# A hybrid attention and gated-linear-attention layer on eight cores: other scrap pairs and transfer order, and one exponential for two maps

## What is computed

```python
h = rms_norm(x, g_pre)
qa, ka, va, za, qb, kb, vb, zb, lr, gate_a, gate_b = split(h @ w_in)   # 5648 columns
# mixer A: 4 heads, two maps m of 64 dims each, causal, ALiBi
p = softmax(q_m k_m^T / 8 - slope * dist)              # m = 0, 1
oa = rms_norm((p_0 - lam * p_1) @ va, g_sub_a) * (1 - lam_init)
ya = (oa * silu(za)) @ w_up_a
# mixer B: gated linear attention, 4 heads, state S (64 x 128)
S_t = diag(alpha_t) S_{t-1} + k_t^T v_t;  ob = q_t S_t  # alpha from lr @ w_alpha
yb = (rms_norm(ob, g_sub_b) * silu(zb)) @ w_up_b
y = sigmoid(gate_a) * ya + sigmoid(gate_b) * yb
out = x + rms_norm(y @ w_out, g_post)
```

## Time and profile before

| | us |
|---|---|
| median of 3 runs | 1646.62 |
| lowest and highest of them | 1643.45, 1820.38 |
| the profiled execution | 1651.65 |
| its span on the slowest core (core 1) | 1650.0 |
| spans of all cores | 1627.0 to 1650.0 |
| PE busy | 1430.6 (87%) |
| ACT busy | 852.6 (52%) |
| DVE busy | 711.4 (43%) |
| POOL busy | 465.3 (28%) |

### The profile page before, as it was taken

One profiled execution on the slowest core, in us unless ns is written; L12 is line 12 of the kernel. 1 busy time (PEld: TensorE's weight loads), 2 busy tenths in 40 slices (PEclk: granted clock), 3 DMA queues, 4 the chain that ended last, 5 costly groups with the idle time before them and its releaser, 6 DMA issues.

```text
span 1650.0 us, 27769 instructions; the slowest of 8 cores (1627.0 to 1650.0 us)
## 1 busy us (share of the span) xinstructions
PE 1430.6 (87%) x10576; PEld 747.7 (45%) x10576; DVE 711.4 (43%) x1449; ACT 852.6 (52%) x1714; POOL 465.3 (28%) x469
## 2 busy tenths in 40 slices
PE   4868687899899997999879998799997999987888
PEld 2324333444445543555445554455543555543443
DVE  3546645653565343542435324353233441242434
ACT  4244343434453555355464665646666657666632
POOL 1024422253225221432204322043311240220342
PEclk9888889999999998999989999999999999999999
DMA  9966487423542335222442223422234312223113
GB/s 286 236 194 179 133 272 233 141 90 115 192 141 90 103 115 179 90 90 93 156 134 66 90 90 122 162 75 76 80 101 153 98 59 76 78 91 115 52 65 115
DMA packets 75437, 207.43 MB, mean 126 GB/s; under 512 B 7984, under 2 KB 26672, under 8 KB 75312
## 3 DMA queue, kind: packets, MB, share of 16 engines
...
## 4 chain that ended last, share of the span: by engine, by line
PE 60%; DVE 12%; ACT 10%; DMA 9%; issue 3%; POOL 3%; SPq 2%; DVEq 0%; POOLq 0%; ACTq 0%
PE ps_q L270 30%; PE ps_f L270 18%; PE ps_oa L270 12%; DMA out<-sb_scr 4%; ACT sb_PT L964 4%; DMA sb_KT<-w_in 3%; DVE sb_scr L841 2%; SPq L364 1%; ACT sb_junk L859 1%; ACT sb_ztmp L613 1%; DVE sb_scr L861 1%; DVE sb_wring L377 1%; DVE sb_rz L990 1%; DMA sb_KT<-w_out 1%; DVE sb_tmpo L992 1%
## 5 line engine op out<-in xcount | busy, mean ns | idle before, releaser
L964 ACT ACTIVATE sb_PT<-ps_q 128x512 bf16<-128x512 f32 (+3 forms) x685 | 363.0, 568 | 254.8 <-PE ps_q L270 170.7
L270 PE MATMUL ps_oa<-sb_V,sb_PT 128*128 128x129 bf16 x4224 | 345.8, 222 | 15.1 <-ACT sb_PT L964 7.5
L270 PEld LDWEIGHTS ps_oa<-sb_V,sb_PT 128*128 128x128 bf16 x4224 | 287.1, 99 | 143.4 <-issue 35.2
L964 ACT ACTIVATE sb_PT<-ps_f 128x512 bf16<-128x512 f32 (+3 forms) x467 | 255.6, 564 | 150.5 <-PE ps_q L270 75.1
L270 PE MATMUL ps_q<-sb_hT,sb_wring 128*128 128x512 bf16 x1040 | 267.3, 391 | 26.0 <-ACT sb_wring L373 8.6
L270 PE MATMUL ps_q<-sb_QT,sb_KT 64*128 64x512 bf16 (+3 forms) x685 | 163.7, 368 | 45.1 <-ACT sb_scr L636 20.5
L270 PE MATMUL ps_f<-sb_hT,sb_wring 128*128 128x512 bf16 x752 | 189.3, 386 | 5.9 <-ACT sb_hT L591 3.7
L809 POOL TENSOR_TENSOR sb_yT<-sb_scr 128x512 bf16<-128x512 f32 x64 | 81.2, 1270 | 397.1 <-DVE sb_scr L807 397.1
L270 PE MATMUL ps_q<-sb_wring,sb_hT 128*128 128x512 bf16 x616 | 166.6, 407 | 21.4 <-DVE sb_szA L614 12.3
L270 PEld LDWEIGHTS ps_q<-sb_hT,sb_wring 128*128 128x128 bf16 x1040 | 94.8, 100 | 141.2 <-issue 62.5
L270 PE MATMUL ps_f<-sb_QT,sb_KT 64*128 64x512 bf16 (+3 forms) x467 | 134.5, 364 | 16.4 <-DVE sb_yT L614 3.1
...
## 6 DMA issues: line engine op xcount, KB each, us to landing
sb_wring<-wsc SPq DMA_DIRECT2D x204, 512.0 KB, 3.6
sb_xb<-x SPq DMA_DIRECT2D x60, 512.0 KB, 4.5
...
out<-sb_scr SPq DMA_DIRECT2D x32, 512.0 KB, 3.3
wsc<-sb_wring SPq DMA_DIRECT2D x30, 512.0 KB, 6.0
...
```

The source lines that it names most:

```text
L270: P.op("pe", lambda e: e.matmul(out=out_, lhsT=lhsT, rhs=rhs, start=start, stop=stop, **kw), reads=reads, writes=writes)
L964: act(lambda e, pp=pp, m=m, c0=c0, b=b, cbias=cbias: e.activation(out=PT[pp][:, m, c0:512], in_=BANK[b][:, c0:512], func=AF.Exp, bias=cbia ...
```

## The change

1. **Pairs.** Group s of the output projection uses pair (s + 2) % 3 instead of s % 3: pairs 2, 0, 1, 2.
2. **Order at the end of `u_f`.** `fin(3)` comes first, then `release(4)`.
3. **Scratch stores.** `wsc` stores are no longer issued behind the conversion, but when the slot is loaded the next time (`owed`), seven pieces later.
4. **Start.** The `cstB` loads go behind six weight pieces, `setup_small` behind K of tile 1; only 8 x loads are issued in the start, the next three and the gpost load at the end of tile 0's attention.
5. **Tile 1.** The core units of the linear attention get cost factor 2 and gaps of 0.5.
6. **Banks.** PSUM is now two pairs of neighbouring banks (q0 with q1, q2 with q3) and one bank f. `bank_take` takes f if two takes have passed since its last, else the one idle for longest. `emit_qk` needs both pairs: a loop runs units on until they are free. Block kb uses one pair for its two maps, the pair idle for longer first.
7. **Exponential.** One activation for each key block reads both banks (2 x 512 columns, on the diagonal 2 x fewer) and writes both maps.

```diff
-        psQ = [PSM(f"q{i}", [128, 512], F32) for i in range(3)]
-        psF = [PSM(f"f{i}", [128, 512], F32) for i in range(2)]
+        psQ = [PSM(f"q{i}", [128, 1024], F32) for i in range(2)]
+        psF = PSM("f", [128, 512], F32)
...
         def bank_take():
-            return idle_banks.pop(0)
+            b = idle_banks[0]
+            if "f" in idle_banks and turn["n"] - turn["f"] >= 2:
+                b = "f"
+            idle_banks.remove(b)
+            turn["n"] += 1
+            turn[b] = turn["n"]
+            return b
...
+        def pair_free(i):
+            return f"q{2 * i}" in idle_banks and f"q{2 * i + 1}" in idle_banks
+
+        def pair_order():
+            age = [max(idle_banks.index(f"q{2 * i}"), idle_banks.index(f"q{2 * i + 1}")) for i in range(2)]
+            return [0, 1] if age[0] < age[1] else [1, 0]
...
-                P.op("sp", lambda e: e.dma_start(out=wsc[pid], in_=base), reads=[wk(n) for n in range(4)], writes=[f"wsc{pid}"],
-                     dma=f"wst{slot}")
+                owed[slot] = lambda: P.op("sp", lambda e: e.dma_start(out=wsc[pid], in_=base), reads=[wk(n) for n in range(4)],
+                                          writes=[f"wsc{pid}"], dma=f"wst{slot}")
...
             slot = i % NPIECE
+            if slot in owed:
+                owed.pop(slot)()
...
-                zg = [scr[:, 2 * (s % 3) + hh, :] for hh in range(2)]
+                zp = 2 * ((s + 2) % 3)
+                zg = [scr[:, zp + hh, :] for hh in range(2)]
...
-                        if s == 3:
-                            u = then(u, lambda: release(4))
...
-            units.append((0.0, lambda: fin(3), False))
+            units.append((0.0, lambda: (fin(3), release(4)), False))
...
-                    first = merge(first, core_units(1.0, 0.0, False) + [z(lambda: None), z(lambda: None), w(0.4, g_tr, 3)])
+                    first = merge(first, core_units(2.0, 0.5, False) + [z(lambda: None), z(lambda: None), w(0.4, g_tr, 3)])
...
+            order = pair_order()
             for kb in kbs:
...
+                pr = order[kb % 2]
                 for m in range(2):
-                    b = bank_take()
+                    b = f"q{2 * pr + m}"
+                    idle_banks.remove(b)
...
-                act(lambda e, pp=pp, m=m, c0=c0, b=b, cbias=cbias: e.activation(
-                    out=PT[pp][:, m, c0:512], in_=BANK[b][:, c0:512], func=AF.Exp, bias=cbias, scale=1.0), [b], [f"PT{pp}_{m}"])
-                bank_give(b)
+                act(lambda e, pp=pp, c0=c0, pr=pr, cbias=cbias: e.activation(
+                    out=PT[pp][:, :, c0:512], in_=psQ[pr][:, :].rearrange("p (m c) -> p m c", m=2)[:, :, c0:512], func=AF.Exp,
+                    bias=cbias, scale=1.0), [f"q{2 * pr}", f"q{2 * pr + 1}"], [f"PT{pp}_0", f"PT{pp}_1"])
+                bank_give(f"q{2 * pr}")
+                bank_give(f"q{2 * pr + 1}")
...
-        consts("sp", "cstB", [(ztmp[:], w_alr, "ztmp"), (lamv_st, lamv_d, "oaf"), (tri[:], tri_d, "tri"), (negm[:], negm_d, "negm"),
-                              (eft[:], ef_d, "eft"), (rmask[:], rmask_d, "rmask")])
         xst["limit"] = 8
         x_load()
-        xst["limit"] = len(xseq)
...
-        setup_small()
+        consts("sp", "cstB", [(ztmp[:], w_alr, "ztmp"), (lamv_st, lamv_d, "oaf"), (tri[:], tri_d, "tri"), (negm[:], negm_d, "negm"),
+                              (eft[:], ef_d, "eft"), (rmask[:], rmask_d, "rmask")])
         run_units(merge(pro_fm(0, "KA", ev_k), a1[5:]))
...
-        consts("sp", "cstC", [(gpost[:], gpost_d, "gpost")])
+        setup_small()
         run_units(tm_chunk([0, 1] if two else [0], QKV[4:6], ev_v))
...
                     if prev:
                         emit_pv(*prev[1])
+                    while not (pair_free(0) and pair_free(1)):
+                        step()
                     emit_qk(t, h, (kb, kb + 1))
...
             run_units(units)
+            if t == 0:
+                consts("sp", "cstC", [(gpost[:], gpost_d, "gpost")])
+                xst["limit"] = len(xseq)
+                x_load()
```

35 lines of the change are left out of this document (22 added, 13 removed).

## The result

| | us |
|---|---|
| changed kernel, median of 4 runs | 1739.03 |
| lowest and highest of them | 1736.83, 1853.67 |
| kernel before, beside it | 1650.41 |
| ratio, with its 95% interval | 1.0547 (1.0488 to 1.0607) |
| predicted; range | 1653; 1600 to 1692 |

In the highest execution of the changed kernel four cores were granted a clock of 0.86 instead of 0.965; the ratios leave such executions out.

The account below looks back on a forecast made before the run. The prediction took TensorE, busy 87% of the span, to bound the kernel. Its terms, -51 + 3 - 13 + 8 + 60 = +7 us, on the median of 1646.6 gave 1653 us, range 1600 to 1692.

Parts of the forecast that it names:

- Store of pair 0/1: Decay gate's exponential at tile changes: no wait for the fourth output store, -51 us; loads behind that store later, +3.
- rival D: Weight loads behind the fourth store: ZB1 late in each of seven tiles, +28 instead of +3, 1678 us; chance 0.06.
- Start: First weight loads: fewer stores and x loads ahead of them shorten PE's idle time, -13 us, bounds 0 and -19.
- seven pieces of lead cover it, so 0: Tile 1: loads waiting for stores just issued out of their slots, in 9 places, were to cost 0.
- Merged exponential: One exponential for both maps: ACT saves 35 us without passing it on; longer latency before PV costs +8 us.
- Rival C: Late tiles: PE does wait for ACT, so ACT's saved 35 us come off, 1618 us; chance 0.04.
- Banks: QK takes all four q banks and waits for evictions still running: +60 us, bounds +10 and +100.
- Single 0.60 to 0.70 plus 0.16, double 1.48: Evictions ahead of QK: us for one eviction plus hand-over, and for a double one; used to price 89 us.
- Where before it stayed open on the fifth bank: Between PV1 and QK: an open chain is now closed, in 51 of the 179 QKs that meet a recently used bank.
- Back come some 14 us of chains: Chains that waited for the youngest bank now meet bank f, giving back some 14 us.
- Rival A: Evictions are covered, as time lost at QK is missing from later waits: bank term +10, 1603 us; chance 0.25.
- Rival B: QK steps of tiles 2 to 7: evictions queue behind long exponentials, bank term +100, latency +18, 1703 us; chance 0.22.

Follow-up runs that it names:

- e5_store: The kernel before with only changes 1 and 2 (shifted scrap pairs, fourth output store ahead of the loads): 1610.29 us, ratio 0.9761.
- e6_start: The kernel before with only changes 3 and 4 (deferred scratch stores, reordered start): 1647.15 us, ratio 0.9992.
- e1_order: The kernel before with changes 1 to 5 only, banks and exponentials as before: 1602.15 us, ratio 0.9712.
- e3_split: The changed kernel with two exponentials for each block again, one for each map, pairs of banks kept: 1727.73 us, ratio 1.0446.
- e16_after_short: The changed kernel with exponentials shortened to two times 64 columns, TensorE's work unchanged: 1682.67 us, ratio 1.0168.
- e11_young: e1_order with QK taking the four youngest idle banks instead of the four oldest: 1639.22 us, ratio 0.9959.
- e9_f1: The changed kernel with bank f given out after one take instead of two: 1750.82 us, ratio 1.0633.
- e12_close: e1_order with open chains closed before each QK, which still takes the four oldest banks: 1673.49 us, ratio 1.0172.
- e18_close_ready: e12_close with every taker of a bank getting the idle one counted as ready first: 1666.99 us, ratio 1.0108.

## Why the prediction was wrong

- **Store of pair 0/1** (-51 + 3 = -48): right in kind, a little large. L655 waits for no store; `e5_store` measured -39, between the lower bound that I gave for the first term (-33) and what I took. No chain of ZB1 came to wait (rival D falls). Whether the store's new place would have done it without the new pairs, as it would by the ring order that the Trainium skill states (DMA: Bandwidth & Descriptors, "Queues, rings and completion order"), no run here shows: both were changed together in every one.
- **Start** (-13): alone it is 0 (`e6_start`), on top of the store -8 (`e1_order` against `e5_store`, change 5 included). Tile 0 did end sooner, by 13.4 us in the median of the cores. The step that failed is "seven pieces of lead cover it, so 0": tile 1 takes 12 us more in `e6_start` and 8 more in `e1_order`. In it a load's wait for its slot's owed store is a wait of SP, 5.3 us each time, and what is queued behind it in order (the fourth output store, the x loads of tile 2) has no seven pieces of lead. I had priced the weights and not the queue.
- **Merged exponential** (+8, bounds -2 and +18): its lengths were right: 1021 ns against 1.03, spacing 0.92 against 0.91, ACT busy 34 us less against 35. 11 us were lost by the medians, but 25 in tiles 2 to 7 (`e3_split`; `e16_after_short` fits it), which is over the upper bound. PV right behind QK pays 9 of them by the matched traces; where the rest lies is open. Rival C falls. By the figures of the Trainium skill (ScalarE: Activation LUTs, "What ACT_TABLE_LOAD costs") its spacing would be an estimated 0.95; 0.92 was measured.
- **Banks** (+60, bounds +10 and +100): this is the term that broke the forecast. 137 us lie between `e1_order` and the changed kernel; less the 11 of merging it measures 126 (112 if merging costs 25). Four steps of it were off.
  - "Single 0.60 to 0.70 plus 0.16, double 1.48" was too cheap. In the matched trace 184 QKs take a bank that a chain or small group used less than 0.8 us of PE work before; PE loses 165 us in front of them, 0.90 each, where I had 89 in 179, 0.50 each. The count was right, the price half. Two things were missing from it. There is a hand-over on both sides: the first reader starts 0.20 behind the end of the chain's last matmul (taken as its start plus 0.21) and QK 0.15 behind the last reader, so that from chain to QK it is typically 0.94 (ACT) or 1.04 (DVE) and for a double eviction 1.76; over all 184 that is some 40 us. And 37 evictions start over 0.3 late, since ACT and DVE work in order (the example at 1296, where the second reader starts 0.66 late); they account for some 45 us.
  - "Where before it stayed open on the fifth bank" I counted as a fresh bank for QK and no more. It is a loss of its own: closing costs 71 us with no fresh bank at QK at all.
  - "Back come some 14 us of chains" was too small: new groups behind QK pay 24.5 less (46.5 against 71.0). This one ran in the kernel's favour.
  - "Some 12 fall into tiles 0 and 1, which weights bound" took these tiles out. They lose too: the first QK of tile 2 comes 17 us later than in `e1_order`.
- **Rival A** (the stall is given back): about a quarter of what QK loses is (24.5 of 111), by chains that meet older banks. In `e11_young` it was half.
- **Rival B** (banks decide, 1703) had the right place and sign, and its bank term of 100 was a fifth under the 126. Its reason was wrong: tanh and square evictions do not queue behind long exponentials. Of the 83 of the 184 that ACT reads first, 4 start over 0.3 late, and with exponentials of 64 columns (`e16_after_short`) the same 184 QKs still lose 164 us.

With the measured terms the sum is 1651.65 - 39 - 8 + 11 + 126 = 1742, against 1740.42 for the profiled execution. It has to come out, as each term is the difference of two runs in a row; it tells nothing of the mechanism. In a second point my own experiments corrected me. I went into them with "QK meets fresh banks" as the whole cause; `e9_f1`, `e11_young` and `e12_close` all missed. A count over every user of a bank (the work missing) ranks the runs for which the expectations give it in the right order, but it predicted 45 us for `e18_close_ready` and got 6.5.
